# Two chained transformer blocks on one core: the first weight tile and x brought in smaller transfers, most constants fetched afterwards, weight splits and preparation of x alternating

## The reference

```
def first_block(x, positions, pre_mix_norm, w_in, ...):
        h = rmsnorm(x, pre_mix_norm[l])
        z = h @ w_in[l]
        conv_in, q_lat, kv_lat, k_rope = z[..., :c1], z[..., c1:c2], z[..., c2:c3], z[..., c3:]
        a, g = jnp.split(conv_in, 2, axis=-1)
        u = a * jax.nn.sigmoid(g)
        u = causal_depthwise_conv(u, conv_w[l], conv_b[l])
...
def rmsnorm(x, g):
    xf = x.astype(jnp.float32)
    y = xf * lax.rsqrt(jnp.mean(xf * xf, axis=-1, keepdims=True) + EPS)
    return (y * g.astype(jnp.float32)).astype(x.dtype)
```

## Time and profile before

| | |
|---|---|
| median of three executions | 2670.63 us (2669.84 to 2671.37) |
| the profiled execution | 2675.11 us |
| its span on the core | 2673.3 us |
| its mean granted TensorE clock | 0.973 |
| PE, DVE, ACT busy | 2542.0, 1659.5, 1274.7 us |

### The profile page before, as it was taken

How to read it: one execution, slowest core, us unless ns; L and a number is a source line. 1 busy time by engine, 2 the same in 40 slices (tenths; PEclk the granted TensorE clock), 3 DMA queues, 4 the chain that set the end, 5 groups by cost and what they waited for, 6 DMA issues and landing times.

```text
span 2673.3 us, 37323 instructions
## 1 busy us (share of the span) xinstructions
PE 2542.0 (95%) x14646; PEld 2211.6 (83%) x14646; DVE 1659.5 (62%) x2164; ACT 1274.7 (48%) x1633; POOL 62.2 (2%) x56
## 2 busy tenths in 40 slices
PE   6998788999999999997999999999899999999997
PEld 5887477888888888886889989887788888888886
DVE  5799565556565654446776436756676767675454
ACT  4446455544444444445453444745554444444342
POOL 0000000000000000000002210000000000000000
PEclk9999789999999999998999999999899999999998
DMA  6554044455555555653553234554355555555553
GB/s 203 174 157 127 0 131 139 160 189 189 187 189 188 188 190 170 205 182 103 196 166 124 84 119 142 177 186 158 111 189 188 188 188 188 188 188 189 178 188 122
DMA packets 235791, 436.23 MB, mean 163 GB/s; under 512 B 14232, under 2 KB 32680, under 8 KB 235552
## 3 DMA queue, kind: packets, MB, share of 16 engines
q1 hardware_dynamic: 232368, 424.02, 49.2%
q0 software_dynamic: 2160, 6.44, 0.8%
q10 hardware_dynamic: 1152, 4.19, 0.4%
HBM read 432.51 MB, written 3.69 MB: 163 GB/s over the span
## 4 chain that ended last, share of the span: by engine, by line
PE 89%; DVE 6%; ACT 2%; issue 1%; DMA 1%; DVEq 0%; SPq 0%; ACTq 0%
PE ps L745 49%; PE ps L748 24%; DVE w_lo L430 2%; PE ps L754 2%; PE ps L756 2%; PE ps L757 2%; DVE ar L1141 1%; PE ps L1165 1%; PE ps L1384 1%; PE ps L1991 1%; PE ps L1997 1%; DMA w_raw<-in_w_in 1%; PE ps L731 1%; PE ps L734 1%; PE ps L733 1%
## 5 line engine op out<-in xcount | busy, mean ns | idle before, releaser
L430 DVE TENSOR_TENSOR w_lo<-w_raw,w_hi 128x1024 fp32r<-128x1024 f32 (+3 forms) x820 | 993.5, 1217 | 794.5 <-ACT w_hi L424 792.7
L745 PE MATMUL ps<-x,w_hi 128*128 128x512 f32 x4320 | 1374.6, 400 | 62.1 <-DVE x L885 28.5
L424 ACT ACTIVATE w_hi<-w_raw 128x1024 fp32r<-128x1024 f32 (+3 forms) x820 | 852.4, 1045 | 945.2 <-PE ps L748 860.1
L748 PEld LDWEIGHTS ps<-x,w_lo 128*128 128x128 f32 x4320 | 820.0, 190 | 195.1
L748 PE MATMUL ps<-x,w_lo 128*128 128x256 f32 x4320 | 855.3, 280 | 0.0
L745 PEld LDWEIGHTS ps<-x,w_hi 128*128 128x128 f32 x4320 | 666.8, 191 | 67.2 <-issue 51.5
L745 PE MATMUL ps<-h,w_hi 128*128 128x512 f32 x1408 | 444.2, 397 | 4.5 <-DVE w_lo L430 4.5
L748 PEld LDWEIGHTS ps<-h,w_lo 128*128 128x128 f32 x1408 | 265.3, 188 | 62.8
L748 PE MATMUL ps<-h,w_lo 128*128 128x256 f32 x1408 | 277.2, 278 | 0.0
L745 PEld LDWEIGHTS ps<-h,w_hi 128*128 128x128 f32 x1408 | 215.1, 189 | 5.2 <-DVE w_lo L430 5.1
L466 ACT ACTIVATE half<-ps 128x512 f32<-128x512 f32 x170 | 99.6, 592 | 103.0 <-PE ps L748 102.8
(11 more groups left out here) (303 smaller groups left out, 1749.8 us busy)
## 6 DMA issues: line engine op xcount, KB each, us to landing
w_raw<-in_w_gate SPq DMA_DIRECT2D x88, 1024.0 KB, 5.2
w_raw<-in_w_up SPq DMA_DIRECT2D x88, 1024.0 KB, 5.2
w_raw<-in_w_down SPq DMA_DIRECT2D x88, 1024.0 KB, 5.1
w_raw<-in_w_in SPq DMA_DIRECT2D x80, 1024.0 KB, 5.1
w_raw<-in_w_out SPq DMA_DIRECT2D x32, 1024.0 KB, 5.1
w_raw<-in_w_xkv SPq DMA_DIRECT2D x8, 1024.0 KB, 5.0
w_raw<-in_w_uq SPq DMA_DIRECT2D x18, 256.0 KB, 3.8
w_raw<-in_w_ukv SPq DMA_DIRECT2D x16, 256.0 KB, 4.0
```

Source lines behind the costliest of these rows:

```text
L424: nc.scalar.activation(w_hi[:, u % HIS, 0:ks.stop - ks.start, cs], w_raw[:, slot(g, j), ks, cs], ACT.Copy)\
L430: nc.vector.tensor_tensor(w_lo[:, slot(g, j), ks, cs], w_raw[:, slot(g, j), ks, cs], w_hi[:, u % HIS, 0:ks.stop - ks.start, cs].bitcast(F3 ...
L745: nc.tensor.matmul(bank, w_h(k, cs), x(k).rearrange("p a n -> p (a n)"), start=(n == 0 and k == 0), stop=False)
L748: ins = nc.tensor.matmul(bank[:, T:2 * T], w_l(k, cs), x(k)[:, 0, :], start=False, stop=(final and k == ks.stop - 1))
```

## The change

SP fetches only the first 16 columns of `cols` ahead of the weights, and the first weight tile as two halves of two chunks with a semaphore each. ACT issues `xt` in five pieces (2, 2, 4, 4 and 4 chunks) and loads the table set for the root at once. ACT and DVE then alternate: split of unit u, preparation of chunks 2u and 2u+1, for u from 0 to 7. POOL waits for the last piece of `xt` and then issues the other 703 columns of `cols` and its own four transfers. The sum over channels moves to after unit 7, the root to after the split of unit 9. DVE waits for the rest of `cols` before the split of unit 8, ACT only when `conv_in` is through.

```diff
@@ load @@
+                    if g.name == "conv_in" and j == 0:
+
+                        for k0, done in ((0, w_first), (HALF, w_loaded[slot(g, 0)])):
+                            for ks, cs, src in gr["src"](i, k0, HALF):
+                                sp.dma_start(w_raw[:, slot(g, 0), k0:k0 + HALF, cs], src).then_inc(done, 16)
+                        continue
@@ split_act @@
-            if u % 2 == 0:
+            if g.name == "conv_in" and u == 0:
+                act.wait_ge(w_first, 16)
+            elif u % 2 == 0 or g.name == "conv_in" and u == 1:
                 act.wait_ge(w_loaded[slot(g, j)], landed(g, i, j))
@@ multiply @@
-                between = (FIRST + 1, sums)
+                between = (at, sums)
@@ sync, gpsimd @@
-            sp.dma_start(cols[:], A["cols"]).then_inc(cols_loaded, 16)
+            sp.dma_start(cols[:, 0:DC], A["cols"][:, 0:DC]).then_inc(cols_first, 16)
...
+            pool.wait_ge(xt_loaded[-1], 16)
+            pool.dma_start(cols[:, DC:NCOL], A["cols"][:, DC:NCOL]).then_inc(cols_loaded, 16)
             pool.dma_start(ident[:], A["ident"]).then_inc(aux_loaded, 16)
@@ scalar @@
-                    stat and (9 if stat[0] in DIRECT else FIRST + 2, lambda: [root(act, name) for name in stat]))
-
-            for k in range(4):
-                act.dma_start(xt[:, 4 * k:4 * k + 4, :], A["xt"][:, 4 * k:4 * k + 4, :]).then_inc(xt_loaded[k], 16)
+                    stat and (9 if stat[0] in DIRECT or done > FIRST + 1 else FIRST + 2,
+                              lambda: [root(act, name) for name in stat]), done)
+
+            for k, (c, last) in enumerate(XP):
+                act.dma_start(xt[:, c:last, :], A["xt"][:, c:last, :]).then_inc(xt_loaded[k], 16)
+            act.preload_act_table_set(LN_EXP)
+            for u in range(DC // 2):
+
+                split_act(act, G["conv_in"], 0, u)
+                if u == 0:
+                    act.wait_ge(cols_first, 16)
+                prep_act(act, "x", xs, gain_of("pre_mix"), lambda c: (xt_loaded[x_piece(c)], 16), "x", None, 2 * u, 2)
+            run_("conv_in", glu_act(act, 0), 3, ["x"], DC // 2)
             act.wait_ge(cols_loaded, 16)
-            ahead_("conv_in")
-            prep_act(act, "x", xs, gain_of("pre_mix"), lambda c: (xt_loaded[c // 4], 16), "x")
-            run_("conv_in", glu_act(act, 0), 3, stat=["x"])
@@ vector @@
+            for u in range(DC // 2):
+                split_dve(dve, G["conv_in"], 0, u)
+                if u == 0:
+                    dve.wait_ge(cols_first, 16)
+                prep_dve(dve, "x", xs, gain_of("pre_mix"), "x", 2 * u, 2)
             dve.wait_ge(cols_loaded, 16)
-            ahead_("conv_in")
-            prep_dve(dve, "x", xs, gain_of("pre_mix"), "x")
             filler = conv_steps(dve)
-            run_("conv_in", filler, 3, stat=["x"])
+            run_("conv_in", filler, 3, ["x"], DC // 2)
@@ tensor @@
-            multiply(pe, G["conv_in"], "x")
+            multiply(pe, G["conv_in"], "x", at=DC // 2)
```

More of the change, by code:

```diff
@@ L355, in build @@
         w_loaded = [sem(f"w_loaded{s}") for s in range(RAW)]
+        w_first = sem("w_first")
         hi_done = sem("hi_done")
@@ L694, in turn, with run @@
                 steps = None
-        def run(eng, split, evict, g, filler=None, fill_from=0, at=None):
-            turn(eng, split, evict, g, 0, None, FIRST + 1, filler, fill_from, at)
+        def run(eng, split, evict, g, filler=None, fill_from=0, at=None, done=FIRST + 1):
+            turn(eng, split, evict, g, 0, None, done, filler, fill_from, at)
             if filler and g.turns > 1:
@@ L703, in run, with multiply @@
                     turn(eng, split, evict, g, i, evict(eng, g, i - 1, g.groups[-1]))
-        def multiply(pe, g, *stats, between=None, filler=None):
+        def multiply(pe, g, *stats, between=None, filler=None, at=FIRST + 1):
             def body(i, first=0, last=g.units):
@@ L825, in build @@
         st_done = sem("st_done")
-        xt_loaded = [sem(f"xt_loaded{k}") for k in range(4)]
+        XP = [(0, 2), (2, 4), (4, 8), (8, 12), (12, 16)]
+        xt_loaded = [sem(f"xt_loaded{k}") for k in range(len(XP))]
+        x_piece = lambda c: sum(c >= last for _, last in XP)
+        cols_first = sem("cols_first")
         cols_loaded, aux_loaded = sem("cols_loaded"), sem("aux_loaded")
@@ L2207, in ahead_, with run_ @@
                 ahead(act, split_act, evict_act, G[name], between, filler)
-            def run_(name, filler=None, fill_from=0, stat=None):
+            def run_(name, filler=None, fill_from=0, stat=None, done=FIRST + 1):
                 run(act, split_act, evict_act, G[name], filler, fill_from,
-                    stat and (9 if stat[0] in DIRECT else FIRST + 2, lambda: [root(act, name) for name in stat]))
-            for k in range(4):
-                act.dma_start(xt[:, 4 * k:4 * k + 4, :], A["xt"][:, 4 * k:4 * k + 4, :]).then_inc(xt_loaded[k], 16)
+                    stat and (9 if stat[0] in DIRECT or done > FIRST + 1 else FIRST + 2,
[9 more added lines that the diff above has]
+            run_("conv_in", glu_act(act, 0), 3, ["x"], DC // 2)
             act.wait_ge(cols_loaded, 16)
-            ahead_("conv_in")
-            prep_act(act, "x", xs, gain_of("pre_mix"), lambda c: (xt_loaded[c // 4], 16), "x")
-            run_("conv_in", glu_act(act, 0), 3, stat=["x"])
             rope_tables_act(act)
@@ L2286, in ahead_, with run_ @@
                 ahead(dve, split_dve, evict_dve, G[name], between, filler)
-            def run_(name, filler=None, fill_from=0, stat=None):
+            def run_(name, filler=None, fill_from=0, stat=None, done=FIRST + 1):
                 run(dve, split_dve, evict_dve, G[name], filler, fill_from,
-                    stat and (9 if stat[0] in DIRECT else FIRST + 2, lambda: refine_dve(dve, *stat)))
+                    stat and (9 if stat[0] in DIRECT or done > FIRST + 1 else FIRST + 2,
+                              lambda: refine_dve(dve, *stat)), done)
             def add_norm(name, src, prep, pgain):
```

## The result

| | before | changed |
|---|---|---|
| median of eight executions, us | 2670.51 (2666.34 to 2675.57) | 2658.4 (2654.73 to 2663.58) |
| the profiled execution, us | 2675.11 | 2654.73 |
| mean granted clock in it | 0.973 | 0.977 |

The ratio is 0.9949, with a 95% interval of 0.9938 to 0.996: 12.1 us or 0.5% faster. The forecast was 2658.0. In the changed kernel the split on ACT is L433 and on DVE L439, x is L882 and L897, the products L754 and L757, the sums L974, the root's first step L1029.

A forecast was written before the change was run, and what follows sets the result against it. PE was taken to bound the kernel nearly everywhere, standing still 23.5 us at the start. 13.3 us earlier start less 0.7 gave 12.6, so median 2670.63 became 2658.0, range 2655.5 to 2663.5.

The forecast's parts named there:

- The start: Program start: half tile lands at 6.8, PE starts at about 10.2 instead of 23.53, 13.3 us earlier.
- from landing to PE: Time from the weights' landing to PE's first product: of the old 8.0 us about 3.4 remain.
- The feed: Units 1 to 7 of the first projection: ACT 2.3 and DVE 2.6 us per unit stay narrowly ahead of PE's 2.79.
- I charged 0.7 us for unit 2: Loss of 0.7 us for unit 2 coming late behind the second tile and for small gaps.
- 12.6: Total forecast gain in us: 13.3 from PE's earlier start less the 0.7 charge.
- The rule that I weighed against the change: Skill page wanting transfers of at least 1 MB, some 2.0 us each; would give median 2660 to 2662; charged nothing.
- Nothing downstream depends on anything but PE's progress, so I carry the whole of it to the end.: After the start: the whole 12.6 us gain lasts to the kernel's end.
- PE starts early and is not fed: Rival, chance 0.19: after an early start PE loses time in the first units; median 2660.6 to 2663.2.
- its two ways: Second tile at 18 instead of 14.6, giving 2660.7; or TensorE's clock staying low one or two units more, 2660.6 to 2663.2.
- Slower: Rival, chance 0.02: DVE waits for held-back constants; unit 8 ready 1.4 us after landing, free until about 35; 2678.0 at 55.
- The half tile is hardly earlier: Rival, chance 0.05: half tile lands at 10 instead of 6.8, PE starts at 13.4, gain 10.1, median 2660.5.
- Given back: Rival, chance 0.04: a later wait on a transfer or DVE's work cancels the gain, leaving 2665.3 to 2675.9.

The follow-up runs named there:

- constants_ahead: Changed kernel with SP fetching all of cols first and POOL issuing its transfers without waiting; half tile landed at 10.2, unit 8 came 4.2 us later.
- x_four: Changed kernel with x in the four old pieces of four chunks; half tile landed at 8.3, unit 8 came 1.9 us later.
- constants_only: Kernel before with only the constants handled as in the change; first tile landed at 11.65, PE started at 19.68, unit 8 came 4.56 us earlier.
- whole_tile: Changed kernel with the first weight tile in one transfer; the tile landed at 9.34, PE started at 12.59, unit 8 came 2.2 us later.
- warm: Changed kernel with ACT's constants wait ahead of run_, plus 20 discarded PE products before unit 0; PE waited 1.55 us for the second tile, unit 8 gained 0.2.
- warm_x_behind: As warm, with x's last two pieces issued by SP behind the second and third weight tiles; unit 8 at 33.51, median of six 2652.66, ratio to before 0.9934.
- constants_late: Changed kernel with POOL's transfers held until PE finished unit 6; cols landed at 36.0, unit 8 was ready 1.4 us later than in the changed kernel.
- no_alternation: Changed kernel with the old order: units 0 to 3 split before all of x, sums after unit 3; unit 8 came 9.3 us later.
- wait_moved: Changed kernel with ACT's wait for the remaining constants ahead of run_, not the rope tables; median of four 2654.75, ratio to before 0.9939.
- alternation_only: Kernel before with the new order alone, transfers as before and no explicit early table load; unit 8 came 4.95 us earlier.
- table_only: Kernel before with one added line loading ACT's table set before the first wait; 0.9 us reached PE's start, 0.3 us unit 8.

## Why the prediction was right

**The start.** The steps held with small margins. Half tile 6.8 forecast, 6.3 measured; second half 10.6 and 9.4; second tile 14.6 and 14.2; from landing to PE 3.4 and 3.3; PE's start 10.2 and 9.59. The missing constants were worth the most: with them ahead the half tile lands at 10.2 (`constants_ahead`), with x in four pieces at 8.3 (`x_four`). Counting packets gave the tile of `constants_only` within 0.1 us and the half tile of `x_four` 0.9 too early.

**The feed.** I charged 0.7 us for unit 2; nothing was lost. DVE had its last chunk ready at 17.35, and PE began it at 17.64. Unit 8 was forecast at 36.5 to 37.5 and came at 35.90. Three terms are mis-sized: the charge by 0.7, the start by 0.6, and the other way unit 0, for which I took the old 4.88 us and which took 5.23. So 12.6 + 0.7 + 0.6 - 0.35 = 13.55, which is the lead of 13.56 that PE had behind unit 8.

**The rule that I weighed against the change** ("DMA: Bandwidth & Descriptors" of the Trainium skill, transfers of 1 MB for what each costs beside its bytes) would have taken 2 to 4 us off. The page's 2.0 us stand in its section on one DMA of the GpSimd path, and its table of sizes is of transfers issued from GpSimd too, while SP and ACT issue the weights and x here. `whole_tile` and `x_four` give the price here: the larger transfers are 2.2 and 1.9 us slower at unit 8, where that rule would have them no slower, and the split itself cost 0.1 us (9.45 against 9.34). These transfers stood in queues behind each other, and no fixed part of 2 us showed.

**The step that failed**: "Nothing downstream depends on anything but PE's progress, so I carry the whole of it to the end." I had followed ACT's moved wait as a wait (never waited for at 100 us) and not as an instruction with a place. It cost 1.3 us by pushing another wait onto a table load. That the sum came out at 12.6 against 12.1 is then partly luck: 1.0 us too little at the start and 1.3 too much behind it.

**The rivals.** "PE starts early and is not fed" did not happen, but its two ways are both seen: `warm` is the tile that comes late, and the low level of the clock over unit 0 costs 2.4 us (unit 0: 5.23 us, in `warm_x_behind` 2.87). "Slower" did not happen, and `constants_late` confirms its rule within 0.1 us. "The half tile is hardly earlier" needs the constants ahead: `constants_ahead` is that case, start 13.50 for the 13.4 given. "Given back" was right in kind, at a place where I found none.

**The parts do not add.** Alone, order, constants and table load give 4.95, 4.56 and 0.3 us at unit 8; undone one at a time from the changed kernel, order, constants, half tile and small x pieces cost 9.3, 4.2, 2.2 and 1.9, which is 17.6 of a gain of 13.75. What lands early is worth nothing while ACT waits in order for something later (`no_alternation`: the first half tile at 6.6, PE's start at 18.91), so each part is worth more with the others.

## What to carry to other kernels

At a start that waits for memory, count what must pass through the DMA engines before the first consumer can run, and move everything else (constants too) behind it; then see that no engine waits in order for a later piece before it handles the first. When two limits lie close together, removing one shows little or nothing: find the next limit from the trace and remove both in one trial. And before a gain of some tenths is believed, compare two traces in which nothing differs up to that point. Last, a wait that is always satisfied is not free: it can move another wait onto an instruction that used to run ahead, so look at which instruction carries which wait after any wait is added or removed.

## What the runs showed of the hardware that I had not expected

- A table load of 1.28 us in front of an ACT instruction takes over part of its waits. In the changed kernel, with one wait more, it ran at 102.89, after the wait, and cost 1.3 us, which `wait_moved` takes back with that one line. In `alternation_only`, with one wait fewer, it ran at 3.33, ahead of the wait.
- In the kernels that start cold PE's first unit cost between 4.17 us (`constants_only`) and 5.26 (`wait_moved`, `constants_late`, `table_only`), and the first two together between 6.96 and 8.44; what decides this was not tested. After 7.5 us of products whose result is thrown away the first took 2.87 and the two 5.65 (`warm_x_behind`). With it the pairs of 512 columns took 0.70 instead of 1.19 us from the first on, the upper of the two levels (2.4 GHz).
- The same transfer of 351.5 KB from POOL landed 6.1 us after its issue in the changed kernel, where the engines moved 389 GB/s from 12.2 to 19 us, and 3.4 us after it in `constants_late`, at 265 GB/s; the slowest of POOL's transfers had taken 9.9 at the program's start.
